# Opening of a one-core decoder kernel: x0 first in the transfer queue, the constants on another queue, the first unit's banks and product order

## The chip, the cores and the metric

The kernel runs on one core of a Trainium2 chip. The metric is the device time of one execution in microseconds, the median of three runs.

## The reference

One inference step of a two-layer trunk, for 512 prompt tokens and 8 x 8 sample tokens that share the weights. What matters for the opening is the first norm and the first projection of layer 0:

```
hp = rmsnorm(xp, norm_mix[i])
hs = rmsnorm(xs, norm_mix[i])
...
proj = h @ w_in
q = proj[..., :HK].reshape(B, T, MLSTM_HEADS, MLSTM_DK)
k = proj[..., HK:2 * HK].reshape(B, T, MLSTM_HEADS, MLSTM_DK) * (MLSTM_DK ** -0.5)
```

After it come the matrix-memory mixer, a gated convolutional feed-forward layer, sliding-window attention and a second feed-forward layer. Everything is float32 at the boundary.

## The kernel before, in words

The 576 tokens (T) are held in five token tiles, x0 to x3 of 128 tokens and x4 with the 64 sample tokens. The model width of 1024 is eight chunks of 128. Activations are kept with features on the partitions, so each x tile is first turned by TensorE: eight 128 x 128 transposes per tile, against an identity matrix that is part of the constants `C`. Every float32 product is made of three float16 products: high by high, high by low and low by high. Activations are split into `hnH` and `hnL`, weights into `wH` and `wL` by `split_act` (L336) on ScalarE and `split_dve` (L342) on VectorE.

The work of each engine is written out by hand in one block per engine, and the engines meet at semaphores. The opening is as follows.

- SyncE (SP) issues the transfers: the first 257 columns of the constants (L2810, semaphore `dI`), x0, x1, x2 (L2813), the first weight block `stage` (L2756), x3, x4 (L2815), three more weight blocks and the parameter rows `rowsF` (L2828). ScalarE issues the three norm rows `rowsD` (L1998).
- TensorE runs eight warm-up products on zeros (L1420), waits for `dI`, and turns x0 to x4 (L1440). After x0 it turns `rowsD` (L1446). Before x2, x3 and x4 it repeats 5, 8 and 6 transposes of x0 that nobody reads (`keep_busy`, L1425). Each x tile goes to a pair of PSUM banks: x0, x1, x2, x3 to the pairs 0, 1, 2, 3, and x4 to pair 0 again, which is why x4 waits for the first of ScalarE's copies out of PSUM (semaphore `xA`).
- VectorE multiplies each turned tile by the norm weight into `z32` (shown as `z`, L2273) and makes the low part `hnL` as `z` less `hnH` (L2278), in the order z0, z1, low 0, z2, low 1, weight split, z3, low 2, z4, low 3, low 4, weight split.
- ScalarE rounds `z` to `hnH` (L2006, semaphore `nrm["hi"]`) and copies the turned tile to `xT` (L2009, `xA`), in the order rounding 0, rounding 1, copy 0, weight split, rounding 2, copy 1, copy 2, rounding 3, rounding 4, weight split, copy 3, copy 4. Then come five squares with row sums (L2025) for the norm.
- TensorE then makes the first of eight units of q and k (`first_unit`, L1459): 48 products of 128 x 128 by 128 x 288, in two halves (`hf`) of 288 tokens. It writes to pair 1. In the first half, tokens of x0 to x2 are read, in the second those of x2 to x4. After it, 22 transposes of `rowsF` (L1473, `ffn_parameters`) and the second unit (L602 in `fm_unit`), then `token_factors` (L1485), the third unit, the gates (L1496) and so on. The units of q and k write to the pairs in `QK_PAIR`; later units depend on how VectorE frees those pairs in the same order.

The norm's own factor (one over the root of the mean square) is applied after the products, so the units don't wait for it.

Of the kernel before, what the change touches and what calls it, by code (L numbers as in the profile page):

```python
# [17 lines left out]
HALF = T // 2  # L18
KD = D // 128
# [3 lines left out]
ROWS = [128, 128, 128, 128, NS]  # L23
# [60 lines left out]
NFIRST = COFF["sel"][0]  # L84


def build(nc, I, O):
# [3 lines left out]
    with ctx:  # L91
# [9 lines left out]
        C = sb("C", [128, NKEPT])  # L101
# [14 lines left out]
        wH = sb("wH", [128, RING, 1024], f16)  # L116
        wL = sb("wL", [128, RING, 1024], f16)
# [138 lines left out]
        PS = ctx.enter_context(nc.psum_tensor("PS", [128, 8, 512], f32))  # L256

        def pair(p):

            return PS[:, 2 * p:2 * p + 2, 0:HALF]  # L260
# [11 lines left out]
        dI, dC, dMask = sem("dI"), sem("dC"), sem("dMask")  # L272
# [3 lines left out]
        hi_ready, lo_ready, unit_used = sem("hi_ready"), sem("lo_ready"), sem("unit_used")  # L276
# [14 lines left out]
        nrm = {s: sem("norm_" + s) for s in ("ps", "rs", "tmp", "hi", "lo")}  # L291
# [21 lines left out]
        xA, x_col, x_diag = sem("x_in_act"), sem("x_col"), sem("x_diag")  # L313
# [34 lines left out]
        def normed(b, k):  # L348
            return (hnH, hnL)[b][:, k, :]
# [1053 lines left out]
        NUM_BANK = (4, 5, 0, 2)  # L1403
        MOUT_PAIR = (0, 3, 1, 2)

        QK_PAIR = (1, 0, 2, 1, 0, 2, 1, 3)
        diag = ntmp[:, :, :].rearrange("p a b -> p (a b)")

        def x_tile(a, tt):
# [1 line left out]

        def x_turned(tt):

            return PS[:, 2 * (tt % 4):2 * (tt % 4) + 2, :].rearrange("p a (k t) -> p (a k) t", t=128)[:, :, 0:ROWS[tt]]

        @block.tensor
        def _(pe):
# [5 lines left out]
            def keep_busy(tt, bank, n):  # L1423
                for k in range(n):
                    nc.tensor.transpose(PS[:, bank, 128 * (k % 4):128 * (k % 4 + 1)],  # L1425
                                        xtok[:, tt, 128 * k:128 * (k + 1)], ident)

            for tt in range(TT):
                if tt == 2:
                    keep_busy(0, 4, 5)  # L1430
                if tt == 3:
                    pe.wait_ge(pd_in, 1)
                    keep_busy(0, 6, 8)
                if tt == 4:
                    pe.wait_ge(xA, 1)
                    keep_busy(0, 0, 6)
                pe.wait_ge(dX[tt], 16)
                r = ROWS[tt]
                for k in range(KD):
                    m = nc.tensor.transpose(PS[:, 2 * (tt % 4) + k // 4, 128 * (k % 4):128 * (k % 4) + r],  # L1440
                                            xtok[0:r, tt, 128 * k:128 * (k + 1)], ident[0:r, 0:r])
                m.then_inc(x_tr, 1)
                if tt == 0:
                    pe.wait_ge(dD, 16 * 3)
                    for k in range(KD):
                        m = nc.tensor.transpose(PS[:, 6, 5 * k:5 * (k + 1)], rowsD[:, 128 * k:128 * (k + 1)],  # L1446
                                                ident[0:5, 0:5])
                    m.then_inc(pd_tr, 1)

            def first_unit():  # L1450

                pe.wait_ge(xA, 2)
                pe.wait_ge(lo_ready, 1)
                for hf in range(2):
                    for b, ready in ((0, nrm["hi"]), (1, nrm["lo"])):
                        pe.wait_ge(ready, 3 + 2 * hf)
                        for k in range(KD):
                            for a in range(2 - b):
                                m = nc.tensor.matmul(pair(QK_PAIR[0])[:, hf, :],  # L1459
                                                     (wH, wL)[a][:, 0, 128 * k:128 * (k + 1)],  # L1460
                                                     normed(b, k)[:, HALF * hf:HALF * (hf + 1)],
                                                     start=(k == 0 and a == 0 and b == 0),
                                                     stop=(k == KD - 1 and b == 1))
                m.then_inc(unit_used, 1)

            def qk_unit(j):
                fm_unit(pe, unit("qk", j // 4, j % 4), range(KD), normed, pair(QK_PAIR[j]), True, True)
# [70 lines left out]
            for c in range(2):  # L1538
                if c:
                    gate_columns()  # L1540
                for u in range(4):
# [4 lines left out]
                    for tt in range(TT):  # L1546
# [3 lines left out]
                        for kk in range(2):  # L1550
                            for a, b in THREE:
                                m = tm_product(tt, (hnH, hnL)[b][:, 2 * u + kk, 128 * tt:128 * tt + rows],
                                               (wH, wL)[a][:, slot, 512 * kk:512 * (kk + 1)],
                                               u == 0 and kk == 0 and (a, b) == THREE[0],
                                               u == 3 and kk == 1 and (a, b) == THREE[2])
# [244 lines left out]
            for c in range(3):  # L1800
                for u in range(4):
# [5 lines left out]
                    for tt in range(TT):  # L1807
# [5 lines left out]
                        for kk in range(2):  # L1813
                            if c == 0 and tt == 0:
                                pe.wait_ge(nrm["lo"], TILES(2) + 2 * u + 2)
                            for a, b in THREE:
                                m = tm_product(tt, (zH, zL)[b][:, 2 * u + kk, 128 * tt:128 * tt + rows],
                                               (wH, wL)[a][:, slot, 512 * kk:512 * (kk + 1)],
                                               u == 0 and kk == 0 and (a, b) == THREE[0],
                                               u == 3 and kk == 1 and (a, b) == THREE[2])  # L1820
# [172 lines left out]

        @block.scalar
        def _(act):
            for rows, src in ((rowsD[0:2, :], I["norm_mix"]), (rowsD[2:4, :], I["norm_ffn"]),
                              (rowsD[4:5, :], I["mlstm_head_norm"])):
                act.dma_start(rows, src).then_inc(dD, 16)  # L1998
# [24 lines left out]
            for tt in range(TT):  # L2023
                x = xtok[0:ROWS[tt], tt, :]
                m = nc.scalar.activation(x, x, ACT.Square, accum_out=xss[0:ROWS[tt], tt:tt + 1])  # L2025
# [32 lines left out]
            for j in range(4):  # L2058
                act.wait_ge(gsem["kt"], j + 1)
                for h in range(MH):  # L2060
                    m = nc.scalar.activation(kw[:, j, 128 * h:128 * (h + 1)], PS[:, 6 + j % 2, 128 * h:128 * (h + 1)],
                                             ACT.Copy, scale=gcol[:, j, 4 + h:5 + h])
# [38 lines left out]
            for h in range(MH):  # L2101
                if h == 0:
                    head_exps(h)
                    act.wait_ge(hsem["ss"], 1)
                    for g in range(MH):
                        m = nc.scalar.activation(ws64[:, g, :], PS[0:NS, 3, NS * g:NS * (g + 1)], ACT.Exp,
                                                 bias=gcol[0:NS, 4, g:g + 1])
# [9 lines left out]
                for tt in range(TT):  # L2117
                    if tt == (TT - 1 if h == MH - 1 else 0):
                        act.wait_ge(hsem["nq"], h + 1)
                    m = nc.scalar.activation(ftok[:, tt, :], num_of(h, tt), ACT.Square,  # L2120
                                             accum_out=stat[:, 0, (tt + 1) % TT:(tt + 1) % TT + 1])
# [4 lines left out]
                for tt in range(TT):  # L2126
                    m = nc.scalar.activation(ftok[:, tt, :], num_of(h, tt), ACT.Copy,
                                             scale=stat[:, 3, (tt + 1) % TT:(tt + 1) % TT + 1])
# [33 lines left out]
            for c in range(3):  # L2162
# [15 lines left out]
                for tt in range(TT):  # L2178
                    tm_done(act, "qkv", c, tt)
                    r = ROWS[tt]  # L2180
# [570 lines left out]
        def _(sp):  # L2751
# [55 lines left out]
                        sp.dma_start(quart[:, q, :].rearrange("p (k c) -> p k c", c=128),  # L2807
                                     quarter(L, p, row, half)).then_inc(landed[q], 16)

            sp.dma_start(C[:, 0:NFIRST], I["const"][:, 0:NFIRST]).then_inc(dI, 16)  # L2810
            def x_load(tt):
                if tt < 4:
                    sp.dma_start(xtok[:, tt, :], I["x_prompt"][0, 128 * tt:128 * (tt + 1), :]).then_inc(dX[tt], 16)  # L2813
                else:
                    sp.dma_start(xtok[0:NS, 4, :], I["x_sample"].rearrange("b t d -> (b t) d")).then_inc(dX[4], 16)  # L2815

            x_load(0)
            x_load(1)
            x_load(2)
            load(unit("qk", 0, 0), win[:, :, 0:128])  # L2820
# [24 lines left out]
            for r in range(2 * PAIRS):  # L2845
                m, _ = done_order(r)
# [173 lines left out]
```

## Time and profile before

| | |
|---|---|
| median of 3 runs | 1197.09 us |
| lowest and highest | 1195.67, 1198.97 us |
| the profiled execution: its own time | 1198.59 us |
| its span, first to last instruction | 1196.8 us |
| mean granted TensorE clock | 0.998 |
| busy: TensorE, VectorE, ScalarE, GpSimd | 1182.0, 863.6, 613.3, 170.3 us |
| HBM traffic | 109.15 MB read, 9.86 MB written |

All times below are microseconds from the start of the span. The profiled execution's own time is 1.8 us over its span. "PE" is TensorE, "PEld" its weight load, "DVE" VectorE, "ACT" ScalarE, "POOL" GpSimd, and "SPq" or "ACTq" the queue on which that engine issues transfers. Transposes appear as MATMUL lines with the identity `C` as an operand. A row of the timeline is a run of like instructions: its start, how long from the first start to the last end, and how many.

### The profile page before, as it was taken

What the parts mean: (1) busy time and instruction counts of PE and PEld (TensorE: products, weight loads), DVE (VectorE), ACT (ScalarE), POOL (GpSimd) and SP (SyncE); (2) the same over time, 40 slices, a digit from 0 to 9 for tenths busy, and PEclk for the clock granted to TensorE, in tenths of its full rate; (3) what the DMA queues carried; (4) which work ended last, traced back from release to release, by engine and by line L of the source; (5) the groups of instructions that cost most, each with busy time, mean ns of one, the idle gap of its engine ahead of it and who ended that gap; (6) DMA issues with size and microseconds to landing.
All of it is one profiled execution on the core that took longest, in us unless ns stands there. A gap on an engine that the chain in (4) does not pass through costs nothing.

```text
span 1196.8 us, 24088 instructions
## 1 busy us (share of the span) xinstructions
PE 1182.0 (99%) x9596; PEld 894.7 (75%) x9596; DVE 863.6 (72%) x1306; ACT 613.3 (51%) x1027; POOL 170.3 (14%) x285
## 2 busy tenths in 40 slices
PE   8999999999999999999999999999999999999998
PEld 6855777777777777777775456677777777787887
DVE  5744677587788878677774579758788888777664
ACT  6322355466555555454435359846555555543432
POOL 1000010002133223000003300000222222110001
PEclk9999999999999999999999999999999999999999
DMA  7642153235645555445546320022755455345663
GB/s 221 242 107 76 52 165 111 76 106 158 160 112 149 124 126 147 128 116 151 146 119 224 94 64 2 2 72 74 200 133 144 111 131 153 92 122 146 154 179 75
DMA packets 197114, 148.60 MB, mean 124 GB/s; under 512 B 5841, under 2 KB 178699, under 8 KB 196450
## 3 DMA queue, kind: packets, MB, share of 16 engines
q1 hardware_dynamic: 181392, 101.72, 29.2%
q0 software_dynamic: 15552, 45.68, 16.6%
q8 instruction: 56, 0.92, 0.3%
q14 instruction: 24, 0.20, 0.0%
q10 hardware_dynamic: 90, 0.09, 0.0%
HBM read 109.15 MB, written 9.86 MB: 99 GB/s over the span
## 4 chain that ended last, share of the span: by engine, by line
PE 87%; DVE 6%; ACT 3%; issue 2%; DMA 1%; SPq 0%; DVEq 0%; ACTq 0%; POOLq 0%
PE PS L602 35%; PE PS L824 17%; PE PS L758 15%; PE PS L618 10%; DVE xT L650 1%; PE PS L1680 1%; DVE P L2706 1%; PE PS L1622 1%; DVE st L2687 1%; PE PS L1881 1%; PE PS L1914 1%; ACT ntmp L658 1%; ACT P L2209 1%; DMA quart<-in_w_ffn_down 1%; DVE wL L342 1%
## 5 line engine op out<-in xcount | busy, mean ns | idle before, releaser
L824 PE MATMUL PS<-hidH,blk 128*128 128x288 f16 x1232 | 227.9, 286 | 0.2 <-ACT val L547 0.2
L342 DVE SCALAR_TENSOR_TENSOR wL<-stage,wH 128x1024 f16<-128x1024 f32 x140 | 170.3, 1221 | 72.5 <-ACT wH L336 72.0
L336 ACT ACTIVATE wH<-stage 128x1024 f16<-128x1024 f32 x140 | 146.3, 1048 | 131.2 <-PE PS L618 56.8
L824 PE MATMUL PS<-hidL,blk 128*128 128x288 f16 x616 | 176.2, 286 | 0.0
L602 PE MATMUL PS<-zH,wH 128*128 128x288 f16 x832 | 169.9, 286 | 0.7 <-DVE zL L663 0.7
L602 PE MATMUL PS<-zL,wH 128*128 128x288 f16 x832 | 169.9, 286 | 0.0
L602 PE MATMUL PS<-zH,wL 128*128 128x288 f16 x832 | 169.9, 286 | 0.0
L824 PEld LDWEIGHTS PS<-hidH,blk 128*128 128x128 f16 x1232 | 120.5, 98 | 30.8 <-ACT val L547 0.5
L602 PEld LDWEIGHTS PS<-zH,wH 128*128 128x128 f16 x832 | 81.2, 98 | 22.0 <-DVE zL L663 1.3
L602 PEld LDWEIGHTS PS<-zL,wH 128*128 128x128 f16 x832 | 81.4, 98 | 20.5
L602 PEld LDWEIGHTS PS<-zH,wL 128*128 128x128 f16 x832 | 81.4, 98 | 20.5
L407 ACT ACTIVATE blk<-quart 128x1408 f16<-128x1408 f32 x48 | 65.5, 1369 | 37.4 <-DMA quart<-in_w_ffn_down 20.1
L602 PE MATMUL PS<-hnH,wH 128*128 128x288 f16 x396 | 81.0, 286 | 1.2 <-issue 1.2
L602 PE MATMUL PS<-hnH,wL 128*128 128x288 f16 x396 | 80.9, 286 | 0.0
L602 PE MATMUL PS<-hnL,wH 128*128 128x288 f16 x396 | 80.9, 286 | 0.0
L413 DVE SCALAR_TENSOR_TENSOR blk<-quart,blk 128x1408 f16<-128x1408 f32 x48 | 77.5, 1619 | 2.2 <-ACT blk L407 2.2
L824 PEld LDWEIGHTS PS<-hidL,blk 128*128 128x128 f16 x616 | 60.3, 98 | 15.0
L520 DVE TENSOR_TENSOR val<-val,PS 128x288 f32<-128x288 f32 x60 | 27.1, 452 | 55.1 <-PE PS L758 27.9
L912 ACT ACTIVATE acc<-G,pff 128x592 f32<-128x592 f32 x44 | 38.7, 879 | 48.2 <-DVE G L1058 48.2
L1256 POOL COPY convO<-G 128x2 f32<-128x2 f32 x44 | 35.3, 802 | 188.7 <-DVE G L1058 188.7
L602 PEld LDWEIGHTS PS<-hnH,wH 128*128 128x128 f16 x396 | 38.1, 98 | 12.7 <-issue 2.1
L602 PEld LDWEIGHTS PS<-hnL,wH 128*128 128x128 f16 x396 | 38.7, 98 | 9.8
(443 smaller groups left out, 2511.8 us busy)
## 6 DMA issues: line engine op xcount, KB each, us to landing
stage<-in_w_ffn_up SPq DMA_DIRECT2D x88, 512.0 KB, 4.2
quart<-in_w_ffn_down SPq DMA_DIRECT2D x32, 704.0 KB, 5.6
stage<-stage POOLq DMA_DIRECT2D x54, 256.0 KB, 4.5
stage<-in_w_mlstm_in SPq DMA_DIRECT2D x24, 512.0 KB, 4.6
stage<-in_w_swa_qkv SPq DMA_DIRECT2D x12, 512.0 KB, 4.6
quart<-quart POOLq DMA_DIRECT2D x8, 704.0 KB, 5.3
quart<-mixed POOLq DMA_DIRECT2D x8, 704.0 KB, 5.6
C<-in_state_mlstm_C POOLq DMA_DIRECT2D x4, 1024.0 KB, 7.2
```

What stands on the lines that cost most here:

```text
L336: nc.scalar.activation(wH[:, slot, :], stage[:, slot, :], ACT.Copy, scale=WSCALE).then_inc(hi_ready, inc)
L342: nc.vector.scalar_tensor_tensor(out=wL[:, slot, :], in0=stage[:, slot, :], scalar=WSCALE, in1=wH[:, slot, :], op0=ALU.mult, op1=ALU.subtr ...
L407: nc.scalar.activation(blk[:, g % RING, 0, :], WEIGHT[j], ACT.Copy, scale=WSCALE).then_inc(hi_ready, 1)
L413: nc.vector.scalar_tensor_tensor(out=blk[:, g % RING, 1, :], in0=WEIGHT[g % BLOCKS], scalar=WSCALE, in1=blk[:, g % RING, 0, :], op0=ALU.mu ...
L520: nc.vector.tensor_tensor(out, a, b, op).then_inc(done, 1)
L602: m = nc.tensor.matmul(out[:, hf, :], w[a][:, slot, 128 * (at + j):128 * (at + j + 1)], xs(b, k)[:, HALF * hf:HALF * (hf + 1)], start=(fir ...
L618: m = nc.tensor.matmul(out, x, w[:, cols], start=first, stop=last, skip_group_check=True)
L650: nc.vector.scalar_tensor_tensor(out=halves(xT[:, m, :]), in0=pair(p), scalar=1.0 / WSCALE, in1=halves(xT[:, m, :]), op0=ALU.mult, op1=ALU ...
L758: m = nc.tensor.matmul(up_psum(bank), w[a][:, at + 128 * k:at + 128 * (k + 1)], x(b, k), start=(start and k == 0 and (a, b) == THREE[0]), ...
L824: m = nc.tensor.matmul(down_bank(g), blk[:, g % RING, a, 128 * k:128 * (k + 1)], (hidH, hidL)[b][:, k, HIDDEN[j], :], start=(k == 0 and (a ...
L912: nc.scalar.activation(acc[:, s, 0:CC], G[:, s, 2:GC], ACT.Identity, bias=pff[:, k, 38 + L:39 + L], scale=pff[:, k, 32 + 3 * L + 2:33 + 3 ...
L1256: nc.gpsimd.tensor_copy(convO[:, L, 0:2, k], G[:, s, SEQ:SEQ + 2])
```

## The change

Three things are changed, all in the opening.

1. SP's first transfer is x0. The constants are issued by ScalarE, ahead of the norm rows, on ScalarE's queue. SP waits for the constants to land (`dI`) before it issues x1 and everything after it.
2. The PSUM pairs are assigned anew. x4 is turned into pair 1 instead of pair 0, after the second of ScalarE's copies instead of the first; the transposes before it that nobody reads write to bank 2. The first unit writes to pair 0 (x0's) instead of pair 1, and waits for the first copy instead of the second. In `QK_PAIR` 0 and 1 are exchanged for all units that used them.
3. The first unit's products are ordered by kind in each half: eight high by high, eight with the low weights, eight with the low activations. Its wait for the low weights comes after the first eight.

```
-        QK_PAIR = (1, 0, 2, 1, 0, 2, 1, 3)
+        QK_PAIR = (0, 1, 2, 0, 1, 2, 0, 3)
+        X_PAIR = (0, 1, 2, 3, 1)
...
-            return PS[:, 2 * (tt % 4):2 * (tt % 4) + 2, :].rearrange("p a (k t) -> p (a k) t", t=128)[:, :, 0:ROWS[tt]]
+            return PS[:, 2 * X_PAIR[tt]:2 * X_PAIR[tt] + 2, :].rearrange("p a (k t) -> p (a k) t", t=128)[:, :, 0:ROWS[tt]]
...
                 if tt == 4:
-                    pe.wait_ge(xA, 1)
-                    keep_busy(0, 0, 6)
+                    pe.wait_ge(xA, 2)
+                    keep_busy(0, 2, 6)
...
-                    m = nc.tensor.transpose(PS[:, 2 * (tt % 4) + k // 4, 128 * (k % 4):128 * (k % 4) + r],
+                    m = nc.tensor.transpose(PS[:, 2 * X_PAIR[tt] + k // 4, 128 * (k % 4):128 * (k % 4) + r],
...
             def first_unit():
 
-                pe.wait_ge(xA, 2)
+                def part(hf, a, b):
+                    for k in range(KD):
+                        m = nc.tensor.matmul(pair(QK_PAIR[0])[:, hf, :], (wH, wL)[a][:, 0, 128 * k:128 * (k + 1)],
+                                             normed(b, k)[:, HALF * hf:HALF * (hf + 1)],
+                                             start=(k == 0 and a == 0 and b == 0), stop=(k == KD - 1 and b == 1))
+                    return m
+
+                pe.wait_ge(xA, 1)
+                pe.wait_ge(hi_ready, 1)
+                pe.wait_ge(nrm["hi"], 3)
+                part(0, 0, 0)
                 pe.wait_ge(lo_ready, 1)
-                for hf in range(2):
-                    for b, ready in ((0, nrm["hi"]), (1, nrm["lo"])):
-                        pe.wait_ge(ready, 3 + 2 * hf)
-                        for k in range(KD):
-                            for a in range(2 - b):
-                                m = nc.tensor.matmul(pair(QK_PAIR[0])[:, hf, :],
-                                                     (wH, wL)[a][:, 0, 128 * k:128 * (k + 1)],
-                                                     normed(b, k)[:, HALF * hf:HALF * (hf + 1)],
-                                                     start=(k == 0 and a == 0 and b == 0),
-                                                     stop=(k == KD - 1 and b == 1))
-                m.then_inc(unit_used, 1)
+                part(0, 1, 0)
+                pe.wait_ge(nrm["lo"], 3)
+                part(0, 0, 1)
+                pe.wait_ge(nrm["hi"], 5)
+                part(1, 0, 0)
+                part(1, 1, 0)
+                pe.wait_ge(nrm["lo"], 5)
+                part(1, 0, 1).then_inc(unit_used, 1)
...
         def _(act):
+            act.dma_start(C[:, 0:NFIRST], I["const"][:, 0:NFIRST]).then_inc(dI, 16)
...
-            sp.dma_start(C[:, 0:NFIRST], I["const"][:, 0:NFIRST]).then_inc(dI, 16)
...
             x_load(0)
+            sp.wait_ge(dI, 16)
             x_load(1)
```

On TensorE, from x3's transposes to the first unit, the order before is this (`x_in_act` is `xA`, `norm_hi` is `nrm["hi"]`, `dX4` the landing of x4; the program's lines are 1 to 8 higher after the change):

```order
L1440 MATMUL PS<-C,xtok 128x128 [waits dX3]
L1440 MATMUL PS<-C,xtok 128x128 x7
L1425 MATMUL PS<-C,xtok 128x128 [waits x_in_act]
L1425 MATMUL PS<-C,xtok 128x128 x5
L1440 MATMUL PS<-C,xtok 128x64 [waits dX4]
L1440 MATMUL PS<-C,xtok 128x64 x7
L1459 MATMUL PS<-hnH,wH 128x288 [waits norm_hi,lo_ready,x_in_act]
L1459 MATMUL PS<-hnH,wL 128x288
```

and in the changed kernel this:

```order
L1426 MATMUL PS<-C,xtok 128x128 [waits x_in_act]
L1426 MATMUL PS<-C,xtok 128x128 x5
L1441 MATMUL PS<-C,xtok 128x64 [waits dX4]
L1441 MATMUL PS<-C,xtok 128x64 x7
L1455 MATMUL PS<-hnH,wH 128x288 [waits norm_hi,hi_ready,x_in_act]
L1455 MATMUL PS<-hnH,wH 128x288 x7
L1455 MATMUL PS<-hnH,wL 128x288 [waits lo_ready]
L1455 MATMUL PS<-hnH,wL 128x288 x7
L1455 MATMUL PS<-hnL,wH 128x288 [waits norm_lo]
L1455 MATMUL PS<-hnL,wH 128x288 x7
```

The places in the order are the same; the wait ahead of the unread transposes is for the second copy (it was for the first), that ahead of the first unit for the first (it was for the second), and the wait for the low weights stands eight products later.

On SP, from the start of the program, the changed kernel has this:

```order
L2821 DMA xtok<-in_x_prompt 128x1024
L2821 DMA xtok<-in_x_prompt 128x1024 [waits dI]
L2821 DMA xtok<-in_x_prompt 128x1024
L2765 DMA stage<-in_w_mlstm_in 128x8x128
L2821 DMA xtok<-in_x_prompt 128x1024
L2823 DMA xtok<-in_x_sample 64x1024
L2765 DMA stage<-in_w_mlstm_in 128x8x128 x3
```

Before, the constants stood ahead of the first row, and there was no wait. They now stand on ScalarE, ahead of the three norm rows.

## Rows read from the trace of the kernel before

**Rows 1.** Windows of the span: us, then busy us (instructions) of each engine, PEclk, DMA, GB/s
```profile
24.63:1196.80 1172.17, 1161.99 (x9453) 879.47 (x9451) 850.19 (x1290) 599.02 (x1010) 164.68 (x273) 1.00 0.45 121
```

**Rows 2.** The chain that ended last, first 40 us: start us, us, what
```profile
1.20 5.83 DMA xtok<-in_x_prompt
...
7.16 1.06 PE PS L1440 x8
...
10.75 1.23 DVE z L2273
...
15.37 1.14 DVE wL L342
...
17.64 1.13 DVE hnL L2278
...
20.09 3.12 PE PS L1459 x24
23.21 1.50 PE PS L1473 x22
24.70 5.99 PE PS L602 x48
```

**Rows 3.** DMA issues, in narrow windows by time: KB, us to landing
```profile
C<-in_const SPq DMA_DIRECT2D x1, 128.5 KB, 2.1
...
xtok<-in_x_prompt SPq DMA_DIRECT2D x1, 512.0 KB, 5.8
...
xtok<-in_x_prompt SPq DMA_DIRECT2D x1, 512.0 KB, 6.6
...
xtok<-in_x_prompt SPq DMA_DIRECT2D x1, 512.0 KB, 7.3
...
stage<-in_w_mlstm_in SPq DMA_DIRECT2D x1, 512.0 KB, 9.0
```

**Rows 4.** Timeline of SP's queue: start us, us, engine line op out<-in xcount
```profile
0.75 0.39 SPq L2810 DMA_DIRECT2D C<-in_const  x1
1.20 1.42 SPq L2813 DMA_DIRECT2D xtok<-in_x_prompt  x3
2.67 0.43 SPq L2756 DMA_DIRECT2D stage<-in_w_mlstm_in  x1
```

**Rows 5.** Timeline of TensorE's products and transposes, 1 to 17 us
```profile
1.21 3.59 PE L1420 MATMUL PS<-hnL 128*128 128x512 f16 x8 [1.21 <-DVE hnL L2256]
...
8.74 1.97 PE L1440 MATMUL PS<-C,xtok 128*128 128x128 f32 x8
...
14.48 0.82 PE L1425 MATMUL PS<-C,xtok 128*128 128x128 f32 x6
15.23 0.70 PE L1440 MATMUL PS<-C,xtok 64*128 64x64 f32 x8
16.84 0.30 PE L1459 MATMUL PS<-hnH,wH 128*128 128x288 f16 x1 [0.91 <-ACT xT L2009]
```

**Rows 6.** Windows of TensorE: us, busy us (instructions), PEclk, DMA, GB/s
```profile
8.75:9.00 0.25, 0.25 (x3) 0.50 0.95 369
...
12.00:12.25 0.25, 0.25 (x3) 0.71 1.14 332
```

**Rows 7.** Timeline of ScalarE, 12 to 23 us
```profile
12.01 1.06 ACT L2006 ACTIVATE hnH<-z 128x1024 f16<-128x1024 f32 x1 [0.61 <-DVE z L2273]
...
13.88 1.05 ACT L336 ACTIVATE wH<-stage 128x1024 f16<-128x1024 f32 x1
...
15.77 1.93 ACT L2009 ACTIVATE xT<-PS 128x1024 f32<-128x1024 f32 x2
...
20.89 1.49 ACT L2009 ACTIVATE xT<-PS 128x1024 f32<-128x1024 f32 x2
```

**Rows 8.** Timeline of VectorE, multiplies of x2 and x4
```profile
13.02 1.22 DVE L2273 TENSOR_TENSOR z<-PS,pd 128x1024 f32<-128x1024 f32 x1
...
18.69 0.68 DVE L2273 TENSOR_TENSOR z<-PS,pd 128x512 f32<-128x512 f32 x1
```

## Prediction

> **What bounds the kernel now.** I read four views, in this order. First the windows of the span: from 24.63 us on, TensorE is busy for 1161.99 of 1172.17 us [rows 1]. So from the second projection unit on, TensorE is the bound, and whatever moves its arrival at 24.6 us moves the end by as much. The change touches only what lies before that point. The reader is to see that this caps the matter: the whole stretch is 2% of the time.
>
> Second, the chain of waits at the start [rows 2]. It runs from the landing of x0 (issued at 1.20, 5.83 us in flight) through x0's transposes, then x1's, and from 10.75 us along VectorE without a gap: multiply z1, residue, multiply z2, and so on to the multiply of x4. Then ScalarE's rounding of x4, the second half of the first unit from 20.09, the parameter transposes from 23.21, the second unit from 24.70. VectorE carries it, and it starts its run only when **x1**, not x0, is transposed.
>
> Third, the transfers. x0 lands 5.8 us after its issue, x1 6.6, x2 7.3, the first weight block 9.0, while the constants took 2.1 [rows 3]; with the issue times [rows 4] that is 7.0, 8.3, 9.5, 11.7 and 2.9 us. So x1 was there at 8.3, and yet its last transpose ended at 10.7: x0's and the norm rows' came first (7.16 to 8.74, 1.58 us), and then x1's took 1.97 us where x0's took 1.06 [rows 5]. The clock columns say why: TensorE stood idle from 4.80 to 7.16, and the granted clock falls from 1.00 (2.4 GHz) to 0.50 (1.2 GHz) just before 8.75 and is on its way back at about 12.1 [rows 6].
>
> Fourth, ScalarE. From 12.01 it runs on end: rounding of x1, copy of x0, split of the first weight block, rounding of x2, copies of x1 and x2 [rows 7]. The copy of x1 ends at about 16.74 (the first of two in 1.93 us), and the first unit starts at 16.84. The unit's order costs little there: its 48 products are 5.83 us at about 0.122 us each, and it took 6.37 (16.84 to 23.21), so 0.54 us of waits lie inside it.
>
> **The change, part by part.**
>
> *Banks and waits.* x4's transposes now use pair 1, whose x1 must have been copied out, so the last TensorE block before the first unit waits for ScalarE's second copy instead of its first. In the trace of before those six keep-busy transposes and x4's eight ran from 14.48 to 15.93 [rows 5], 1.45 us hidden ahead of the second copy. Now all 14 stand behind it. The first unit waits only for the first copy, but it is queued behind x4's transposes on TensorE, so its shorter wait buys nothing. Cost: 1.45 us, less the 0.54 of waits inside the unit, plus 0.1 for the step from the copy to the first of them: **+1.0 us**, measured from the end of the copy of x1.
>
> *High products first.* With the start at 16.74 + 0.1 + 1.45 = 18.3 in old times, the unit finds everything ready: the low weights (VectorE's split ended at 16.5 [rows 2]), the low part of x2 by the time the third eight begin (ready at 18.8 [rows 2], wanted at 18.3 + 2 x 0.97 = 20.2), rounding of x4 at 20.05 against 21.2. So the new order is worth at most the 0.54 already counted; by itself nothing more. The multiply of x4 started at 18.69 [rows 8] and now needs x4 transposed at 18.3: just covered, price 0 to 0.3 us in the low part, which is read last. The parameter transposes need the copies of x3 and x4, done at 22.38 [rows 7] against 24.2 now.
>
> *Constants on ScalarE's queue.* SP issues x0 at 0.75 instead of 1.20, 0.45 us sooner. ScalarE issues the three norm rows one transfer later, about 0.5 us; they are read after x0's transposes. The cost is 0, covered by TensorE's warm-up, which lasts to 4.80 anyway [rows 5].
>
> *x0 alone.* x0's landing moves from 7.0 to somewhere between 2.9 (the time of the small transfer) and 6.55 (its own 5.8 from 0.75). Until 4.80 it gains nothing more. I take x0 ready at 4.8: its transposes and the norm rows' end at 6.38, z0 (1.22 us, as z2 [rows 8]) before 8.0. All of that ends in a wait: **x1** is late next.
>
> *x1 waits for the constants*, and behind it on SP wait x2, all four weight blocks, x3, x4 and the parameter rows. The constants land between 2.87 (alone, as before) and 6.55 (as slow as x0 was). I take 3.2, nearest to their own row, since only x0 travels beside them. Then x1 is issued at 3.25. Its flight lies between 2.1 us (the constants' row) and 6.6 (its own). I take 5.4: like x0 it is now the first of a train, 5.8 less the 0.4 us that 128 KB take at 369 GB/s [rows 6], the constants no longer being ahead of it. It lands at 8.65, 0.35 later than before: the wait costs x1's issue 1.6 us, and the shorter train gives 1.2 back.
>
> *From x1 to the copy.* TensorE is idle from 6.38 to 8.7, nearly as long as the 2.36 us that preceded the fall before. The transposes of x1 then cost 1.06 us at 2.4 GHz or 1.97 at 1.2; no row says which, so I take the middle, 1.5. z1 starts at 8.7 + 1.5 + 0.05 = 10.25, **0.5 sooner** than 10.75. x2, one place up the train, lands at 3.7 + 6.6 = 10.3, and its eight transposes are done by 12.4 even at 1.2 GHz, while z2 is wanted at 12.5 (before: 13.02 [rows 8]). The first weight block, issued at 4.2, lands between 11.5 and 13.2 and is wanted at 13.4 (before 13.88 [rows 7]). So ScalarE's run starts 0.5 sooner and its second copy ends 0.5 sooner.
>
> **Sum**: +1.0 - 0.5 = +0.5 us. Against the profiled execution's own 1198.59 (span 1196.8) that is 1199.1; the median of the runs shown is 1.5 lower, 1197.09, and against it the forecast is **1197.6**. A difference of 0.3%, 3.6 us, is about what a measurement of this kernel can tell from none: single runs spread from 1195.67 to 1198.97.
>
> **A rule against it.** The trace has x0 taking 5.8 us and the constants 2.1, both on one queue [rows 3], and cannot show what two queues do. The Trainium skill (DMA: Bandwidth & Descriptors, "Issuing engines are not separate DMA queues") says that transfers started by different engines run on the same 16 DMA engines and interleave, so a second issuer saves only sequencer time. By that rule the constants are slowed by x0 rather than passed around it; by it the sum would lie between mine and that of the fourth rival.
>
> **The rivals.**
>
> 1. *x1 comes early.* If x1's flight is 4.3 us, having less ahead of it, it lands at 7.55 and z1 starts at 8.7 at full clock, 2.0 sooner. More is impossible: x2 would have to beat 9.5 and the weight block 11.7. The second copy ends 2.0 sooner: 1.0 - 2.0 = -1.0, **1196.1**. For: x1 is the head of its train. Against: x0 was that too, and took 5.8.
>
> 2. *The low clock returns inside the first unit.* TensorE now has a new idle stretch, from the end of x3's transposes (before: about 14.5) to the second copy at 16.2. If a spell like that of 8.7 to 12.1 falls on the unit, 3.4 us run at half rate and lose 1.7; with x1's transposes slow as well, 1.0 + 1.7 = +2.7, **1199.8**. Against: 1.7 us is shorter than the 2.36 that brought the fall.
>
> 3. *Nothing gets sooner.* x1's transposes slow and x1 at 8.7: z1 starts at 10.75 as before, and only the moved transposes remain: +1.0, **1198.1**. It is the case in which putting x0 first does not do what it says.
>
> 4. *The constants arrive with x0, and the wait holds all of SP's queue.* Landing at 6.55, x1 is issued at 6.6, lands at 12.0, z1 starts between 13.2 and 14.1, 2.5 to 3.3 late: +3.5 to +4.3, **1201.0**. It decides against the kernel by over 0.3% from an x1 landing at about 12.1, and makes it slower at all from one at 7.7 to 8.6. Against: their 128 KB took 2.1 us with x0 issued 0.45 behind.
>
> **How the numbers follow.** Forecast 0.56; rival 1, 0.15; rival 2, 0.10; rival 3, 0.10; rival 4, 0.05; and 0.04 for a gain over 3.6 us by something outside the sum, since nothing on this path can give it. The first four cases lie within 0.3% (0.91); of rival 2, 0.01 may go over. The range reaches from rival 1, less 0.8 for the scatter of a median of few runs, to rival 3 and part of rival 2: 1195.3 to 1199.3.
>
> **What would show it.** Right: x0's transposes at 4.8, then an idle stretch of about 2 us that ends with x1 at 8 to 9; VectorE's unbroken run from about 10.3; keep-busy and x4's transposes starting after the copy of x1, at about 16.3; the first unit without gaps, and the second at about 25.2. Wrong: x1 landing before 7.7 (rival 1) or after 10 (rival 4); a granted clock of 0.50 beside the lines of the first unit (rival 2); a start of x4's transposes that is not the moment of ScalarE's second copy; or any difference in TensorE's time after 24.7.

## The result, and the profile after

| | before | after |
|---|---|---|
| median | 1197.50 us (20 runs) | 1199.91 us (20 runs) |
| lowest and highest | 1195.67, 1201.12 | 1199.02, 1203.83 |
| ratio, 95% interval | | 1.0020 [1.0012, 1.0027] |
| the profiled execution: own time, span | 1198.59, 1196.8 | 1201.10, 1199.3 |
| parameter transposes start (L1473; L1481 after) | 23.14 | 25.84 |

The change makes the kernel 2.4 us slower by the medians. That is clear of zero and under 0.3%. The forecast was 0.5 us slower, 1197.6, in a range from 1195.3 to 1199.3: the sign held, the size and the range did not. One execution of `ahead_of_copy` (1531.48 us, mean granted clock 0.752) and one of before (1986.46 us, 0.574) were in a slow state, and the ratios below leave them out.

The timeline of TensorE in the changed kernel answers to [rows 5] (start, length, engine, line, operation, and the wait before it):

```profile
5.02 1.09 PE L1441 MATMUL PS<-C,xtok 128*128 128x128 f32 x8 [0.23 <-DMA C<-in_const]
6.05 0.66 PE L1447 MATMUL PS<-C,rowsD 5*128 5x5 f32 x8
8.65 1.97 PE L1441 MATMUL PS<-C,xtok 128*128 128x128 f32 x8 [1.94 <-DMA xtok<-in_x_prompt]
...
16.74 0.87 PE L1426 MATMUL PS<-C,xtok 128*128 128x128 f32 x6 [2.09 <-ACT xT L2018]
17.55 0.70 PE L1441 MATMUL PS<-C,xtok 64*128 64x64 f32 x8
18.19 1.70 PE L1455 MATMUL PS<-hnH,wH 128*128 128x288 f16 x8
19.68 2.13 PE L1455 MATMUL PS<-hnH,wL 128*128 128x288 f16 x8
21.59 1.38 PE L1455 MATMUL PS<-hnL,wH 128*128 128x288 f16 x8
22.81 1.14 PE L1455 MATMUL PS<-hnH,wH 128*128 128x288 f16 x8
```

Three things are to be seen. x0 is turned from 5.02, two microseconds sooner than in [rows 2], and then TensorE waits 1.94 us for x1. The unread transposes and x4's stand behind ScalarE's copy of x1, after 2.09 us of idleness, and the first unit starts at 18.19 instead of 16.84. And its first products take up to 2.13 us for eight, where later ones take 1.14. The windows of TensorE give the reason (us, busy, granted clock, DMA share, GB/s; they answer to [rows 6]):

```profile
18.00:19.00 1.00, 1.00 (x11) 0.82 1.07 265
19.00:20.00 1.00, 1.00 (x6) 0.50 1.26 151
20.00:21.00 1.00, 1.00 (x6) 0.50 0.96 51
21.00:22.00 1.00, 1.00 (x6) 0.50 1.12 239
22.00:23.00 1.00, 1.00 (x10) 0.97 1.29 312
```

The clock fell to 1.2 GHz inside the unit, after the idle stretch of 2.09 us. In the chain of waits (start, length) the unit stands with 7.66 us where 5.9 would do:

```profile
0.76 4.22 DMA C<-in_const
...
5.00 3.61 DMA xtok<-in_x_prompt
...
8.65 1.98 PE PS L1441 x8
...
10.66 1.24 DVE z L2282
...
15.78 0.92 ACT xT L2018
...
18.25 7.66 PE PS L1455 x48
25.91 1.49 PE PS L1481 x22
```

The issues, in narrow windows by time, answer to [rows 3]: beside x0 the constants took 4.2 us instead of 2.1, and x1, issued only at 5.0, took 3.6.

```profile
xtok<-in_x_prompt SPq DMA_DIRECT2D x1, 512.0 KB, 4.0
C<-in_const ACTq DMA_DIRECT2D x1, 128.5 KB, 4.2
...
xtok<-in_x_prompt SPq DMA_DIRECT2D x1, 512.0 KB, 3.6
```

**One number carries the comparison.** In the profiles of both kernels the rest is alike: 1198.59 - 23.14 = 1175.45 us before, 1201.10 - 25.84 = 1175.26 after. Over all 17 profiles of this study, of every variant, an execution's own time is the start of the parameter transposes plus 1175.0 to 1176.2 us in 15; of the two exceptions, `banks_undone` is explained below and `rows_early_before` (1177.1) is not. So I read each variant by that start, and its runs by their median and their interval. By an estimate from the medians, the usual start is about 22.2 before (1197.5 - 1175.3) and 24.6 after. Both profiles of the changed kernel (25.8 and 25.9) are later than that, and so is the profile of before (23.1).

### The profile page after: what moved, and what is told of

Same layout as the page of the kernel before. It is cut to its first block, busy times and chain, and to the rows that moved or that the text cites. A ratio compares the mean times of both kernels' runs of the same rounds, so it can differ in the third digit from the quotient of the medians.

```text
span 1199.3 us, 24088 instructions
## 1 busy us (share of the span) xinstructions
PE 1183.9 (99%) x9596; PEld 895.4 (75%) x9596; DVE 863.1 (72%) x1306; ACT 614.1 (51%) x1027; POOL 173.7 (14%) x285
## 4 chain that ended last, share of the span: by engine, by line
PE 89%; DVE 5%; ACT 3%; issue 1%; DMA 1%; DVEq 0%
PE PS L602 35%; PE PS L824 19%; PE PS L758 15%; PE PS L618 10%; DVE xT L650 1%; PE PS L1688 1%; PE PS L1455 1%; DVE P L2715 1%; PE PS L1630 1%; DVE st L2696 1%; PE PS L1889 1%; PE PS L1922 1%; ACT ntmp L658 1%; ACT wH L336 1%; ACT P L2218 1%
## 5 line engine op out<-in xcount | busy, mean ns | idle before, releaser
L1256 POOL COPY convO<-G 128x2 f32<-128x2 f32 x44 | 38.4, 874 | 187.2 <-DVE G L1058 187.2
```

The lines of the kernel that those rows point to most:

```text
L1256: nc.gpsimd.tensor_copy(convO[:, L, 0:2, k], G[:, s, SEQ:SEQ + 2])
```

## The experiments

The theories after the result: **(A)** x4's transposes behind the second copy; **(B)** the low clock inside the first unit, which came after the idle stretch ahead of them; **(C)** what holding SP's queue until the constants have landed makes late. Each kernel ran 11 or 12 times beside 23 to 33 runs of before; `before_again` and `after_again` ran once. One interval is about 1.1 us to either side, so differences of 1 us between single kernels are seldom clear by the times alone. Kernels that were measured side by side can also be compared directly; the others only by their ratios to before.

**Each part alone.** `transfers_only` is the kernel before with these edits:

```
+            act.dma_start(C[:, 0:NFIRST], I["const"][:, 0:NFIRST]).then_inc(dI, 16)
-            sp.dma_start(C[:, 0:NFIRST], I["const"][:, 0:NFIRST]).then_inc(dI, 16)
             x_load(0)
+            sp.wait_ge(dI, 16)
```

> The kernel before with only the transfers changed: x0 first, the constants on ScalarE's queue, x1 behind the constants. The banks, x4's place and the product order stay. The theory (the slow stretch comes from x4's transposes standing behind the second copy): x1 lands near 8.6 as in the changed kernel, x1's transposes run at 1.2 GHz, VectorE's run starts at about 10.7 as before, and the parameter transposes start near 23.1, so the time equals the kernel before within 0.5 us. The rival (the held-back transfers cost the 2.4 us): 2 us or more above before.

Measured: 1199.06 against 1197.94 us, ratio 1.0006 [0.9997, 1.0015]. x1's flight was 3.6 us here too, and the parameter transposes started at 22.96. By the interval it is anything from 0.4 us faster to 1.8 slower: undecided. Against `order_only` below, which was measured beside it, it is 0.85 us slower by the medians.

`banks_only`:

```
-        QK_PAIR = (1, 0, 2, 1, 0, 2, 1, 3)
+        QK_PAIR = (0, 1, 2, 0, 1, 2, 0, 3)
+        X_PAIR = (0, 1, 2, 3, 1)
...
-                    pe.wait_ge(xA, 1)
-                    keep_busy(0, 0, 6)
+                    pe.wait_ge(xA, 2)
+                    keep_busy(0, 2, 6)
...
             def first_unit():
-                pe.wait_ge(xA, 2)
+                pe.wait_ge(xA, 1)
```

> The kernel before with only the banks and waits changed: x4 in pair 1 behind the second copy, the first unit in pair 0. The theory: TensorE idles about 2 us before x4's transposes, the granted clock falls to 0.50 inside the first unit, the parameter transposes start about 2.7 us late at 25.8, and the time is 2.4 us above before. Without a fall of the clock (the moved transposes alone) it would be 1.0 above. The rival (the transfers are to blame): equal to before.

Measured: 1199.52 against 1197.94, ratio 1.0008 [0.9999, 1.0017]. That is the 1.0 us expected for the moved transposes alone, though the interval just reaches zero; and in the profile there is nothing of a low clock. There x0 landed at 5.1 and x1 at 7.0, and the first transposes ran at full rate:

```profile
5.24 1.26 PE L1441 MATMUL PS<-C,xtok 128*128 128x128 f32 x8 [0.45 <-DMA xtok<-in_x_prompt]
6.44 0.65 PE L1447 MATMUL PS<-C,rowsD 5*128 5x5 f32 x8
7.02 1.09 PE L1441 MATMUL PS<-C,xtok 128*128 128x128 f32 x8
...
14.58 0.87 PE L1426 MATMUL PS<-C,xtok 128*128 128x128 f32 x6 [1.23 <-ACT xT L2010]
15.39 0.71 PE L1441 MATMUL PS<-C,xtok 64*128 64x64 f32 x8
```

The block behind the copy is there, 1.45 us long (14.58 to 16.03). The start at 22.01 is earlier than in the profile of before, and its own time, 1197.75, is the lowest of its eleven. So single profiles differ by over a microsecond for reasons that are not the edit. That had to be looked at (below).

`order_only` has only the new order of the first unit's products.

> The kernel before with only the product order of the first unit changed. All theories: the unit starts at 16.84 as before, since the second copy holds it, and its last products wait for the same low parts; within 0.3 us of before.

Measured: 1198.21 against 1197.94, ratio 0.9999 [0.9990, 1.0008], start at 23.03. The order costs and gains nothing that can be seen, as forecast.

**The low clock in the unit.** `gap_filled` is the whole change with

```
                 if tt == 4:
+                    pe.wait_ge(xA, 1)
+                    keep_busy(0, 0, 8)
+                    keep_busy(0, 0, 8)
                     pe.wait_ge(xA, 2)
                     keep_busy(0, 2, 6)
```

> The changed kernel with 16 transposes more that nobody reads, in the idle stretch before the second copy (they wait for the first copy only). Nothing is taken away. If the fall of the clock costs the time: the granted clock stays at 1.00 beside the first unit, its 48 products take 5.9 us where they took 7.66, the parameter transposes start near 24.1, and the time falls by 1.8 us to about 0.7 above before. If the place of x4's transposes alone costs it: unchanged, 2.4 above before.

Measured: 1199.95, ratio 1.0015 [1.0006, 1.0024]:

```profile
15.54 2.56 PE L1426 MATMUL PS<-C,xtok 128*128 128x128 f32 x22
18.04 0.70 PE L1444 MATMUL PS<-C,xtok 64*128 64x64 f32 x8
...
24.66 1.56 PE L1484 MATMUL PS<-C,rowsF 40*128 40x40 f32 x22
```

The unit runs from 18.68 to 24.66, 5.98 us, with the clock up, and the median did not move from 1199.91. Two things weaken what follows from it. x3 was turned late in this execution, so that the 16 added transposes began only at 15.54 and ran some 0.4 us past the end of the copy of x1 (16.84); the edit then also delays. And 1.0006, what the forecast of this run asks for, is the lower end of the interval. So (B) is unlikely to be the main cost of the median, but it is not excluded.

`after_again` is the whole change again, for a second profile.

> The changed kernel once more, for another profile of it. If its slow first unit of 7.66 us belongs to some executions only: 5.9 to 6.0 us here, the parameter transposes at 24.0 to 24.6, behind the landing of their rows near 24.0, and an own time of that start plus 1175.5. If it belongs to the kernel: 7.66 again and 25.8.

Measured: the unit starts at 18.21 and takes 7.66 us again, start at 25.87, own time 1202.08. Of the 20 timed runs of the changed kernel, the nine with a mean granted clock of 0.997 (that of both profiles) have a median of 1201.10, and ten of the other eleven lie between 1199.0 and 1200.4. A mean tells how long the clock was recorded low, and not where: the profile of `gap_filled` has 0.997 too, with a unit at full rate. So in the changed kernel more low clock goes with more time, and the runs with less of it still stand about 2 us above before; how often the spell falls on the first unit is not shown.

**The floor.** `banks_undone` is the whole change with the banks and waits of before: transfers and product order only.

> The changed kernel with its banks and the places of the waits undone: x4 is turned into pair 0 behind the first copy, the first unit writes to pair 1; the transfers and the product order stay changed. The theory (two separate costs: x1 held behind the constants, about 1.0 us, and x4's transposes behind the second copy, about 1.2): the time falls to about 1.0 us above before, the first unit starts right after the copy of x1. The rival (only the clock inside the first unit counts): the same time as the kernel with the gap filled, 1.8 above before.

Measured: 1199.94 against 1197.98, ratio 1.0017 [1.0008, 1.0026]: not 1.0 but 2 us slower, though (A) and (B) are gone. The timeline of TensorE names the wait that I had priced at nothing:

```profile
22.16 1.14 PE L1454 MATMUL PS<-hnL,wH 128*128 128x288 f16 x8
24.09 1.57 PE L1480 MATMUL PS<-C,rowsF 40*128 40x40 f32 x22 [0.79 <-DMA rowsF<-in_ffn_conv_b]
...
26.52 0.69 PE L602 MATMUL PS<-hnH,wH 128*128 128x288 f16 x2
```

The unit is done by 23.3, and TensorE waits for the **parameter rows**, the last of SP's transfers ahead of the loops. Their last issue stood at 16.33; in the changed kernel at 16.25 and 16.17, and in two executions of before at 15.47 and 14.66. This execution also had a low spell in the second unit (0.69 where 0.41 is usual, granted clock 0.50 from 27 to 29), 1.67 us by the chain; it is the exception that is explained.

```profile
16.33 7.71 DMA rowsF<-in_ffn_conv_b
...
24.09 1.57 PE PS L1480 x22
25.66 7.66 PE PS L602 x48
```

Two things keep this from being the whole answer. By the last update of their semaphore in the traces, the rows landed at 24.05 here, but at 22.10 and 22.44 in the two profiles of the changed kernel and at 22.50 in `gap_filled`, there 2.2 to 3.7 us before the unit had ended; in the two profiles of before they landed at 22.56 and 22.21. And `transfers_only` differs from this kernel in the product order alone and came out at 1.0006, with its rows down by 22.7: the difference of 1.3 us between the two (their intervals overlap) is not explained, since the order by itself changed nothing.

`rows_early_undone` is `banks_undone` with

```
-            for u in range(1, 4):
-                load(unit("qk", 0, u), win[:, :, 128 * u:128 * (u + 1)])
+            load(unit("qk", 0, 1), win[:, :, 128:256])
             for rows, src in ((rowsF[0:32, :], ...
...
+            for u in range(2, 4):
+                load(unit("qk", 0, u), win[:, :, 128 * u:128 * (u + 1)])
```

> The changed kernel with its banks undone, and SP issuing the parameter rows ahead of the third and fourth weight blocks instead of behind them. If the late parameter rows are what holding SP's queue costs (they landed at 24.0 us there, TensorE waiting 0.8 us for them): the parameter transposes follow the first unit at about 23.1 without a wait, and the time falls from 2.2 above before to 1.0 to 1.4 above. If it is x1's landing alone: unchanged.

Measured: 1198.36 against 1197.75, ratio 1.0003 [0.9994, 1.0012]. The last rows are issued at 10.63, and the transposes follow the unit without a wait:

```profile
22.46 1.14 PE L1454 MATMUL PS<-hnL,wH 128*128 128x288 f16 x8
23.53 1.57 PE L1480 MATMUL PS<-C,rowsF 40*128 40x40 f32 x22
```

By the ratios that is 1.6 us less than `banks_undone`, from one reordering of SP's queue, though the two intervals touch. So late rows can cost over 1 us where the unit ends early; how often they do is not shown.

`rows_early_before` does the same to the kernel before.

> The kernel before with the parameter rows ahead of the third and fourth weight blocks. If they are the last to arrive in many of its executions too: 0.3 to 0.8 us faster than before. If not: equal to before.

Measured: 1196.68 against 1197.75, ratio 0.9993 [0.9984, 1.0003]. It may be a small gain; it is not shown. (Its profile is the slowest of its eleven executions, 1200.76.) But it is the kernel that `rows_early_undone` has to be held against, since the rows are early in both: 1198.36 against 1196.68, side by side. The held transfers still cost 1.7 us by the medians (1.0 by the means) with the rows out of the way.

`rows_early_after` does it to the whole change.

> The whole change with the parameter rows ahead of the third and fourth weight blocks. If x4's transposes behind the second copy set the first unit's end at 24.1 or later, as by the trace, the rows at 24.0 are hidden under it: unchanged within 0.4 us, 2 above before. If the rows are the only cost: 1 us faster than the changed kernel.

Measured: 1199.58 against 1197.75, ratio 1.0021 [1.0012, 1.0030]: unchanged, as (A) says; late rows are not what the changed kernel waits for. With `rows_early_undone` beside it at 1198.36, the banks and their waits cost 1.2 us by the medians (1.6 by the means). In its profile the unit ran at full rate (5.99 us) and the parameter transposes started at 23.51.

**What (A) is made of.** `ahead_of_copy` adds to `rows_early_after`

```
                 if tt == 4:
+                    pe.wait_ge(xA, 1)
+                    keep_busy(0, 0, 8)
+                    keep_busy(0, 0, 8)
                     pe.wait_ge(xA, 2)
-                    keep_busy(0, 2, 6)
```

> The changed kernel with the parameter rows early (their wait is out of the way), 16 unread transposes ahead of the wait for the second copy and none behind it. If the block behind the copy sets the first unit's start: 0.82 us less stands there, and with no idle stretch the clock stays up; the parameter transposes start about 0.8 us sooner after the copy of x1 (7.0 behind its end instead of 7.4 to 9.1), and the time falls from 2.2 above before to 0.9 to 1.4 above. If the place doesn't matter: unchanged.

Measured: 1198.88 against 1197.32, ratio 1.0011 [1.0002, 1.0019]; by the ratios 1.2 us less than `rows_early_after`, though the two intervals overlap.

```profile
14.12 1.91 PE L1426 MATMUL PS<-C,xtok 128*128 128x128 f32 x16
16.62 0.71 PE L1443 MATMUL PS<-C,xtok 64*128 64x64 f32 x8 [0.59 <-ACT xT L2020]
17.26 1.15 PE L1457 MATMUL PS<-hnH,wH 128*128 128x288 f16 x8
```

Behind the copy only x4's eight are left, 0.64 us instead of 1.45, and the unit runs at full rate. The 0.8 expected for the block is met; whether the clock gave a part of the 1.2 is open, since the unit of `rows_early_after` ran at full rate in its profile too.

**Which half of the transfers.** `no_x1_wait` is the whole change without `sp.wait_ge(dI, 16)`.

> The changed kernel without SP's wait for the constants ahead of x1; all else stays. If holding the queue costs the 1 us: x1 is issued at about 1.2 and lands between 6 and 7 instead of 8.6, and the time falls to about 1.2 us above before. If the constants' slower landing on ScalarE's queue costs it: they land later still beside three tiles (over 5 us), x0's transposes wait for them, and the time stays about 2.3 above.

Measured: 1199.70 against 1197.98, ratio 1.0017 [1.0008, 1.0026]. x1 was issued at 1.2 and took 5.4 us, as in the first case; the constants took 4.5; and the norm rows, now behind the constants on ScalarE's queue and beside three tiles, landed only at 7.3:

```profile
5.32 1.09 PE L1441 MATMUL PS<-C,xtok 128*128 128x128 f32 x8 [0.61 <-DMA C<-in_const]
7.38 0.67 PE L1447 MATMUL PS<-C,rowsD 5*128 5x5 f32 x8 [0.97 <-DMA rowsD<-in_mlstm_head_norm]
...
16.07 0.87 PE L1426 MATMUL PS<-C,xtok 128*128 128x128 f32 x6 [2.23 <-ACT xT L2018]
16.87 0.70 PE L1441 MATMUL PS<-C,xtok 64*128 64x64 f32 x8
17.51 1.15 PE L1455 MATMUL PS<-hnH,wH 128*128 128x288 f16 x8
```

Neither expectation fits whole: x1 landed at 6.6, 2 us sooner than in the changed kernel, but behind the late norm rows its multiply started only 0.7 us sooner (9.98 against 10.66). With x4's block in place, the start is 23.50 and the gain over the changed kernel is not clear. This trace also tells something of (B): TensorE was idle for 2.23 us here, longer than the 2.09 of the changed kernel, and yet the unit ran at full rate. The idle stretch alone does not bring the low clock; what does is open. `x1_unheld` leaves the wait out too, and has the banks of before:

> The kernel before with the constants on ScalarE's queue and the new product order, no wait ahead of x1, and the old banks. If the hold is what costs: equal to before or up to 0.4 us faster, since x0 and x1 are issued 0.45 us sooner. If the second queue costs: 1 us above before, with the constants landing after 5 us.

Measured: 1198.25 against 1197.98, ratio 1.0005 [0.9995, 1.0015]. Parameter rows last issued at 14.43, start at 22.66 after a wait of 0.55 us for them. Against `banks_undone` (1.0017, measured beside it) the wait on SP's queue is the only difference: it costs 1.7 us by the medians. With it x1's landing moves from 6.9 to 8.9, and the rows' last issue by 1.9 us.

`busy_x1` is `banks_undone` with 16 more transposes that nobody reads between the norm rows and x1:

```
                     m.then_inc(pd_tr, 1)
+                    keep_busy(0, 7, 8)
+                    keep_busy(0, 7, 8)
```

> The kernel before with the transfers and the product order changed, and 16 transposes that nobody reads between the norm rows and x1, where TensorE idles from about 6.9 to 8.6. If a low clock on x1's transposes is half of what the transfers cost: those eight take 1.06 us, VectorE's second multiply starts at 9.8 instead of 10.1 to 10.7, and the time falls by 0.3 to 0.9 us against the same kernel without them, to about 0.4 above before. If the landing of x1 alone costs it: unchanged, 1.0 above.

Measured: 1199.12, ratio 1.0005 [0.9996, 1.0015]. x1's transposes took 1.04 us at full rate, and in this execution TensorE then waited 1.45 us for the parameter rows, until 23.97: there the gain is eaten by the next wait.

**Why executions of before differ.** `before_again` is the kernel before, for a second profile.

> The kernel before once more, for another profile of it. The theory says that its first profile was a late one: x0's flight is about 4 us here instead of 5.8, and the parameter transposes start between 21 and 23 us; in any case the execution's own time is that start plus 1175.5 us, as in nine of the ten profiles so far.

Measured: own time 1198.26, start at 23.29, so the start plus 1174.97. x0's flight was 4.2 us, x1's 5.0, and yet nothing was gained:

```profile
5.58 1.94 PE L1440 MATMUL PS<-C,xtok 128*128 128x128 f32 x8 [0.78 <-DMA xtok<-in_x_prompt]
7.45 1.01 PE L1446 MATMUL PS<-C,rowsD 5*128 5x5 f32 x8
8.39 1.97 PE L1440 MATMUL PS<-C,xtok 128*128 128x128 f32 x8
10.15 1.27 PE L1425 MATMUL PS<-C,xtok 128*128 128x128 f32 x5
11.22 1.91 PE L1440 MATMUL PS<-C,xtok 128*128 128x128 f32 x8
```

Every transpose up to 13 us took the time of 1.2 GHz. In `banks_only` they took that of 2.4 GHz from x1 on. With x1 landed at 6.7 here and 7.0 there, VectorE's second multiply started at 10.40 here and at 8.51 there.

`longer_warm_up` is `rows_early_before` with ten warm-up products instead of eight (`range(8)` to `range(10)`).

> The kernel before with the parameter rows early and ten warm-up products instead of eight (they end at about 5.6 instead of 4.8). If the first low stretch of the clock, on the transposes of x0 to x2 in five of the profiles, comes from the idle time before x0 and costs 1 to 2 us: the transposes run at full rate from 5.7 and the time falls to 1 us or more under before. If the stretch has its own timing: no faster than the kernel with the rows early alone, 0.4 under before, or slower by up to 0.4, since x0 waits for the warm-up.

Measured: 1196.99 against 1197.32, ratio 0.9995 [0.9986, 1.0004]; all eleven executions within 1.9 us of each other. In its profile TensorE has no idle time ahead of x0, and the first transposes are fast:

```profile
5.75 1.06 PE L1440 MATMUL PS<-C,xtok 128*128 128x128 f32 x8
6.74 0.65 PE L1446 MATMUL PS<-C,rowsD 5*128 5x5 f32 x8
7.33 1.09 PE L1440 MATMUL PS<-C,xtok 128*128 128x128 f32 x8
...
21.28 1.56 PE L1473 MATMUL PS<-C,rowsF 40*128 40x40 f32 x22
```

Its start of 21.28 is the earliest of all profiles, 1.9 us under the first of before. Over the runs it is the best candidate, but the interval still holds 1: that it beats before is not shown.

## Why the prediction was wrong

- **The bound**: right. When TensorE is through with the opening sets the end, and the rest is the same to about 0.6 us either way in 15 of 17 profiles.
- **Banks and waits, +1.0**: right in mechanism, and about right in size. The block behind the copy is 1.45 us (16.74 to 18.19), and the unit's own waits are gone. `banks_only` gives 1.0 us by the ratio, the pair `rows_early_after` and `rows_early_undone` 1.2 to 1.6.
- **High products first, 0**: right by `order_only`; that `transfers_only` and `banks_undone` differ is left open.
- **x0 alone**: the path was right, the landing of x1 luck. x0 is turned at 5.02, and x1 is late next, at 8.61 (forecast 8.65). But the constants took 4.2 us, not 2.4, and x1 3.6, not 5.4, and the two errors cancelled. The rule of the Trainium skill (DMA: Bandwidth & Descriptors, "Issuing engines are not separate DMA queues"), that transfers of different engines run on the same DMA engines and interleave, agrees with this trace: the constants on ScalarE's queue took 4.2 us with x0 beside them, and 2.1 ahead of it on SP's queue.
- **The step that failed**: the transfers' term of the sum, "ScalarE's run starts 0.5 sooner and its second copy ends 0.5 sooner". The runs show a cost in its place: 0.7 us by the ratio of `transfers_only` (undecided by itself), and 1.7 us by the medians in each of the two pairs measured side by side (`banks_undone` and `x1_unheld`; `rows_early_undone` and `rows_early_before`, whose executions scatter over 4.8 us, so that the second pair is only just clear of nothing by the means). It went wrong in three places.
  - *x1's transposes.* I took the middle between the two clock levels. In both profiles of the change they took 1.97 us, z1 started at 10.66 and 10.68 against 10.75, and the gain was 0.1.
  - *"0.35 later than before".* That held x1's new landing against 8.26, from one late execution. The seven other profiles without the wait on SP's queue have x1 at 6.6 to 7.1, and all nine with it at 8.5 to 8.9. So the wait makes x1 some 1.4 to 2.3 us late, and takes away the executions in which VectorE's second multiply starts early: at 8.5 to 9.4 in three profiles without the wait, nowhere before 9.99 with it.
  - *"and behind it on SP wait x2, all four weight blocks, x3, x4 and the parameter rows".* I named the rows and then costed only x1. Of the parameter transposes I asked whether the copies of x3 and x4 were done, and not whether their own rows had landed. In three profiles TensorE did wait for them, 0.55 to 1.45 us. In both profiles of the changed kernel it did not: this floor is real, but it is not what set their time.
- **Rival 2** (the low clock inside the unit, +2.7) is what both profiles of the change show, to the tenth: 25.84 - 23.14 = 2.70. Against the sum, which put the start at 23.14 + 0.5 = 23.64, the profile is 2.2 late: 0.4 from z1 (10.66 for 10.25) and 1.8 from the low clock in the unit, which the sum held at nothing. I held against rival 2 that 1.7 us of idleness is shorter than the 2.36 before; the idle stretch was 2.09, and `no_x1_wait` shows that its length does not decide. It got one chance in ten. How much of the median rests on it is open: `gap_filled` did not move it.
- **The reference point**: the profile of before that I worked from had x0 in flight for 5.8 us; the other five profiles with the constants and x0 in this order at the queue's head have 3.9 to 4.6. It was itself 1.1 us over the median. A loss against late landings is smaller than one against usual ones, and taking 1.5 us off for the median did not mend that. Banks at 1.0 and transfers at 0.7 add up to 1.7 us by the two single parts, where the whole is 2.4; the rest lies within the intervals.

## What to carry to other kernels

When a wait is put into a transfer queue, go through everything behind it to the last transfer, and ask for each who reads it and when. Then look in the changed kernel's own trace which of them TensorE waited for: a floor that shows in a variant need not be the one that holds the kernel itself. Hold a variant against a kernel that differs from it only in the part that is tested: `rows_early_undone` looks almost free beside before (1.0003), and by the medians costs 1.7 us beside `rows_early_before`. And for a stretch of 20 us at the start of a kernel, look at several profiles of the same program before taking any duration from one.

## What the runs showed of the hardware

- The granted clock's column reads 1.00 until the first change that the trace recorded, whatever the true level. In `before_again` eight transposes took 1.97 us at 8.39, as long as at a granted 0.50 in the profile of before, and the column says 1.00 throughout (us, busy, clock, DMA share, GB/s):

```profile
9.00:10.00 1.00, 1.00 (x7) 1.00 1.10 434
...
12.00:13.00 1.00, 1.00 (x7) 1.00 1.20 238
13.00:14.00 1.00, 1.00 (x11) 1.00 1.15 347
```

  At a start the durations of equal instructions tell the level (0.21 us from the start of one transpose to that of the next here, 0.11 in `longer_warm_up`), not the column.
- The warm-up products of 512 columns took 0.40 to 0.43 us from start to start in every profile, but for the last one in `gap_filled` (0.36), while a 288-column product took 0.122 at a granted 2.4 GHz; by that, 512 columns would take 0.22, an estimate. So TensorE was at 1.2 GHz during the warm-up, and the step up came between 4 and 13.5 us, differently from one execution to the next.
- 128 KB of constants took 2.1 to 2.2 us at the head of SP's queue, with x0 issued 0.45 us behind; with one 512 KB tile issued at the same moment from another engine, 4.0 to 4.4; with three tiles, 4.5. In the kernels with the wait on SP's queue, a 512 KB tile took 3.5 to 4.1 us (x0 and x1). Without it, x1 behind x0 took 5.0 to 6.6.
